# Prompt attention of a decoder step on one core: scaled scores from ScalarE, and another place for the weights' low part

## What is computed

```
z = (q @ k^T) / sqrt(HEAD_DIM) + bias
log_keep = where(mask, log_sigmoid(-z), 0)
suffix = cumsum(log_keep, reversed) - log_keep
attn = where(mask, exp(log_sigmoid(z) + suffix), 0)
o = attn @ v
proj = u @ w_in          # q and gate for all 16 heads, k and v from s @ w_k, s @ w_v
```

## Time and profile before

| | |
|---|---|
| Median of three runs | 1843.4 us |
| The profiled execution: its time | 1843.44 us |
| Its span from first to last instruction | 1841.7 us |
| TensorE busy | 1746.1 us, 95% of the span |
| VectorE busy | 1137.3 us, 62% |
| ScalarE busy | 822.4 us, 45% |
| Granted TensorE clock, mean | 0.983 |

### The profile page before, as it was taken

One profiled execution on the slowest core, in us unless ns is written; L12 is line 12 of the kernel. 1 busy time (PEld: TensorE's weight loads), 2 busy tenths in 40 slices (PEclk: granted clock), 3 DMA queues, 4 the chain that ended last, 5 costly groups with the idle time before them and its releaser, 6 DMA issues.

```text
span 1841.7 us, 35650 instructions
## 1 busy us (share of the span) xinstructions
PE 1746.1 (95%) x14063; PEld 1674.6 (91%) x14063; DVE 1137.3 (62%) x1917; ACT 822.4 (45%) x1246; POOL 230.8 (13%) x173
## 2 busy tenths in 40 slices
PE   6999999999999999996898999999998999999997
PEld 5999999999999999994898989989987888899996
DVE  4766555676567422229578788787876666642366
ACT  4434444344445222224255655655664555622343
POOL 2000000000000000011232222322321111001111
PEclk9999999999999999998999999999998999999997
DMA  8322332332322332335222222222213777622465
GB/s 247 107 83 78 91 89 82 91 93 78 91 80 69 87 90 86 85 106 179 83 82 58 76 63 64 76 63 58 86 48 110 210 229 221 196 75 86 134 182 189
DMA packets 293526, 197.98 MB, mean 107 GB/s; under 512 B 8379, under 2 KB 267579, under 8 KB 293307
## 3 DMA queue, kind: packets, MB, share of 16 engines
q1 hardware_dynamic: 290632, 187.36, 34.9%
q0 software_dynamic: 2720, 8.78, 1.3%
q10 hardware_dynamic: 68, 0.41, 0.1%
HBM read 180.55 MB, written 15.97 MB: 107 GB/s over the span
## 4 chain that ended last, share of the span: by engine, by line
PE 79%; DVE 10%; issue 5%; ACT 4%; DMA 1%; SPq 0%; ACTq 0%; POOL 0%; DVEq 0%
PE PS L720 22%; PE PS L722 22%; PE PS L721 22%; PE Z L983 2%; PE Z L720 1%; PE Z L722 1%; PE Z L721 1%; PE Z L993 1%; DVE WS L1657 1%; DMA xin<-in_x_prompt_dram 1%; DVE T L1953 1%; DVE T L1954 1%; PE Z L1017 1%; ACT T L1387 1%; PE Z L1176 1%
## 5 line engine op out<-in xcount | busy, mean ns | idle before, releaser
L720 PE MATMUL PS<-U,WS 128*128 128x272 f32 x3680 | 1078.1, 293 | 28.4 <-DVE U L1920 14.0
L722 PE MATMUL PS<-U,WS 128*128 128x272 f32 x3680 | 1067.6, 290 | 0.0
L721 PE MATMUL PS<-U,WS 128*128 128x272 f32 x3680 | 1065.1, 289 | 0.0
L720 PEld LDWEIGHTS PS<-U,WS 128*128 128x128 f32 x3680 | 697.1, 189 | 42.5 <-issue 22.3
L721 PEld LDWEIGHTS PS<-U,WS 128*128 128x128 f32 x3680 | 696.9, 189 | 0.9
L722 PEld LDWEIGHTS PS<-U,WS 128*128 128x128 f32 x3680 | 696.1, 189 | 0.0
L1657 DVE TENSOR_TENSOR WS<-raw,WS 128x1024 fp32r<-128x1024 f32 (+1 forms) x223 | 298.0, 1337 | 368.3 <-ACT WS L1208 365.8
L1208 ACT ACTIVATE WS<-raw 128x1024 fp32r<-128x1024 f32 (+1 forms) x225 | 230.7, 1025 | 479.4 <-PE PS L722 478.8
L633 POOL TENSOR_TENSOR raw<-raw,GN 128x1024 f32<-128x1024 f32 x80 | 158.0, 1975 | 583.5 <-DMA raw<-in_b_w_in_dram 486.7
L642 POOL COPY T<-T 128x544 f32<-128x544 f32 x2 | 1.7, 862 | 611.9 <-ACT T L1347 562.3
L1407 ACT ACTIVATE U<-T 128x256 fp32r<-128x256 f32 (+1 forms) x64 | 31.9, 499 | 88.5 <-DVE T L1972 88.5
(11 more groups left out here) (286 smaller groups left out, 2070.8 us busy)
## 6 DMA issues: line engine op xcount, KB each, us to landing
raw<-in_a_w_in_dram SPq DMA_DIRECT2D x80, 512.0 KB, 3.8
raw<-in_b_w_in_dram SPq DMA_DIRECT2D x64, 512.0 KB, 4.1
raw<-in_a_w_out_dram SPq DMA_DIRECT2D x32, 512.0 KB, 3.9
KPG<-in_cache_k_dram SPq DMA_DIRECT2D x64, 256.0 KB, 3.0
raw<-in_b_w_out_dram SPq DMA_DIRECT2D x32, 512.0 KB, 3.9
VPG<-in_cache_v_dram SPq DMA_DIRECT2D x60, 256.0 KB, 3.0
RAW<-in_b_w_out_dram SPq DMA_DIRECT2D x12, 512.0 KB, 4.7
scratch_x<-T POOLq DMA_DIRECT2D x16, 272.0 KB, 3.5
```

Of the source, the lines that this page charges most:

```text
L720: pe.matmul(psum, w_hi, x_hi, start=first, stop=False)
L721: pe.matmul(psum, w_hi, x_lo, start=False, stop=False)
L722: return pe.matmul(psum, w_lo, x_hi, start=False, stop=last)
```

## The change

Two edits. On ScalarE, `exp_logits` gets a fourth operation: behind Abs, an Identity with the same scale and bias writes z to T[:, 0] and raises `z_out`. VectorE's `scaled` is gone, with its wait for `z_abs`. In VectorE's `step`, `low` moves from in front of `mask_weights` to behind `at_rest` and in front of `sp_rest`.

```diff
-                nc.scalar.activation(T[:, 1, q], Z[:, 0, s % 2, q], ACT.Abs, scale=SCALE,
-                                     bias=BIAS[:, k * GRP + g:k * GRP + g + 1]).then_inc(z_abs, 1)
+                bias = BIAS[:, k * GRP + g:k * GRP + g + 1]
+                nc.scalar.activation(T[:, 1, q], Z[:, 0, s % 2, q], ACT.Abs, scale=SCALE, bias=bias).then_inc(z_abs, 1)
+                nc.scalar.activation(T[:, 0, q], Z[:, 0, s % 2, q], ACT.Identity, scale=SCALE, bias=bias).then_inc(z_out, 1)
                 act.wait_ge(z_abs, n + 1)
...
-            def scaled(k, g, s):
-                n = k * 16 + 4 * g + s
-                q = slice(FIRST_Q[s], SEQ)
-                dve.wait_ge(z_abs, n + 1)
-                if n:
-                    dve.wait_ge(l_ready, n)
-                V.tensor_scalar(T[:, 0, q], Z[:, 0, s % 2, q], SCALE, BIAS[:, k * GRP + g:k * GRP + g + 1],
-                                ALU.mult, ALU.add).then_inc(z_out, 1)
-
...
                 if before:
                     exponent(*before)
-                if s == 0:
-                    scaled(k, g, 0)
-                if next_unit is not None:
-                    low(D0 + next_unit, next_unit % 2)
-                if before:
                     mask_weights(*before)
                 if s == 1 and (k or g):
                     head_out(*((k, g - 1) if g else (k - 1, GRP - 1)))
                 softplus(k, g, s)
                 if before:
                     at_rest(*before)
+                if next_unit is not None:
+                    low(D0 + next_unit, next_unit % 2)
                 sp_rest(k, g, s)
-                if s < 3:
-                    scaled(k, g, s + 1)
```

## The result

The changed kernel takes 1861.94 us (four runs, 1861.46 to 1862.86 us), the kernel before 1845.43 us on the same chip (four runs, 1842.26 to 1849.64 us). The ratio is 1.0085 (slower by 0.85%), 95% interval 1.0063 to 1.0106. The forecast was 1851.8 us with a range of 1837 to 1861: the sign was that of the sum, the size was about half, and the time lies outside the range. The two profiled executions have spans of 1841.7 and 1861.1 us, 19.4 us apart. Where those lie is read from them.

A forecast was written before the change was run, and what follows sets the result against it. The prediction took TensorE, 95% busy, as the bound, with 25.0 us of its waits on VectorE's order. Terms 4.0 + 3.5 + 2.4 - 1.5 = +8.4 us on the median 1843.4 gave 1851.8 us, range 1837 to 1861.

The forecast's parts named there:

- The ceiling of 29.1 us: TensorE's whole idle time in the steps from 924 to 1392 us, claimed as the most any gain there could be.
- `scaled` goes: VectorE loses 64 operations, 37 us of its time; in steps s > 0 the next operation begins up to 0.75 us earlier.
- Identity comes: ScalarE's added copy delays Ln and softplus by 0.35 to 0.55 us and gives ScalarE 27 us more work.
- rival 4: Identity on ScalarE needs another table, loaded twice in each of 64 steps: 2007 us at worst, chance 0.02.
- `low` moves, the open wait: VectorE idles 0.5 us per step before the mask; chain from `exponent` to `sp_rest` grows from 4.17 to 4.41 us.
- The fold: GpSimd's fold moves with `low` onto softplus and `at_rest`: 0 to 1.9 us lost per unit, minus 0.55 saved.
- two-step units: Eight units holding two steps: first wait gone, later ones added by folds, net +0.5 us each, +4.0 us in all.
- gate units: Units ending a gate strip: `low` now stands in the open behind the mask, `later` waits about 1 us; +3.5 us in all.
- the steps s = 0: 16 steps where Abs to Ln is no longer covered by `low` and a fold can fall in: +2.4 us.
- Loads ... priced at nothing: Weight slots come free up to 3 us later, but some 2.5 us of reserve before `high` was taken to absorb it.
- Rival 3: Weight loads become the bound: some 20 of 55 units slip by 0.7 us, +14 us on top, 1866 us; chance 0.08.
- Rival 1: Faster: folds fall beside VectorE's chain or do not stop softplus, -7.7 us, 1835.7 us; chance 0.2.

## Why the prediction was half right

- **The bound and the ceiling.** TensorE's path and the waits for VectorE were the right place. The ceiling of 29.1 us was one of idle time at the granted clock and left out that the clock can fall behind waits.
- **`scaled` goes.** Right that it starts `exponent` earlier: L909 fell from 9.8 to 2.5 us with this edit alone. The move alone does as much (2.3 us), and both give 0.5. What the edit is worth was seen too small: alone it gives 10 us, where only the 0.75 us in front of the next `exponent` was weighed.
- **Identity comes.** Estimated at 0.35, 0.45 and 0.55 us of ScalarE's chain; starts are 0.36, 0.46 and 0.57 us apart (the unit of 1047.44, 1060.31 and 1125.25 us). ScalarE got 20.5 us in the steps where 27 stood. No table load came with it, so rival 4 falls; the Trainium skill's filler rule (ScalarE: Activation LUTs, Table sets) agrees.
- **`low` moves, the open wait.** Priced at 0.5 us, seen as 0.52 us of idle time (0.83 us at 1063.14 us, where `high` stands in front on ScalarE). The chain was put at 4.41 us; in a unit without a fold on it, it takes 4.75 us (1061.88 to 1066.63). The name of the wait changed as described, L901 from 4.1 to 21.4 us against "20 or more". But L923 was to fall under 4 us and stayed at 9.7.
- **The fold.** Right in mechanism and place. Softplus's operations with both inputs in SBUF are stopped as `tensor_tensor` is. The row, with the fold beside it, is below. Over the steps the mean of `low` fell from 1763 to 1340 ns, that of softplus's first operation rose from 515 to 677, `sp_rest` from 577 to 830. But as waits the folds cost TensorE no more than before (22.0 us of idle time against 23.3, each kernel against its run without folds); what they added came through the clock.

```profile
1079.84 2.14 DVE L1945 SCALAR_TENSOR_TENSOR T<-T 128x256 f32<-128x256 f32 x1 [1.19 <-ACT T L1392]
```
```profile
1079.78 1.91 POOL L633 TENSOR_TENSOR raw<-raw,GN 128x1024 f32<-128x1024 f32 x1 [7.60 <-DMA raw<-in_b_w_in_dram]
```

  By the Trainium skill (SBUF — State Buffer, Who interferes with whom) two SBUF inputs are enough; the trace agrees, 2.14 us for 0.42.
- **The sum.** In terms of waits it was too high by about 3 us, with its largest term right. Added up over the timeline, the waits in two-step units went from 19.9 to 24.4 us, +4.5 against +4.0. The gate units' own waits and the `rest` behind them gave +0.7 against +3.5, the steps s = 0 +0.6 against +2.4, and a wait of 0.7 us made by a fold in the first head went (against -1.5). All waits in the steps: +5.0 us against +8.4. The gate units' wait itself was seen rightly: put at about 1 us, it is 0.73 to 0.94 us in the seven of them. That the total comes near the forecast's is in part luck: it is the difference of Identity's gain of 10 us and a move that costs 26 beside it, and neither was priced as such.
- **The step that failed first: the clock.** The sum has no term for TensorE's speed, and took the earlier trace rows's 1.00 as given. 13.7 us more at the lower level are up to 6.8 us, of 7.3 us of busy time, more than the added waits (4.7). The row to warn of it was there: the 2.17 us wait of the earlier trace rows is followed by the only such stretch in the steps before.
- **The step that failed second: the queue.** "Loads ... priced at nothing" looked at the reserve of the weight slots only. What stands behind the waiting load on SyncE, the first key pages, wasn't asked. It costs 5.7 us of wait and, by the profiles, 6.3 us of span; the run with early key pages gives 5.5 us of time back. Rival 3 was near this place with another mechanism, and that one did not come: VectorE's `low` waited for `high` for 0.0 us in the changed kernel.
- **Added up.** Ahead of the steps +1.2 us, idle time in them +4.7, busy time +7.3, behind them +6.3: 19.5 against 19.4 us of span. The +1.2 belongs to neither edit: the first step's `qk` starts anywhere from 919.6 to 922.9 us in the runs here. The medians of the comparison are 16.5 us apart; the clock's falls differ from execution to execution, and the split is that of the profiled one.
- Rival 1 (faster) needed less than 0.5 us of each fold on the chain. The means of the mask, softplus's three operations and both low parts, less those of the kernel without folds, add up to 1.1 us for each fold; in the kernel before it was 0.3 us, and `low` took 0.5.

## To carry to other kernels

An operation that frees a buffer starts what comes after it: moving it moves the load, everything queued behind that load on the same queue, and the next engine's work on the tile, so follow it until it meets the critical chain again. Where two engines exclude each other, look first for the order in which they meet; here one wait on GpSimd is worth 12 us, and taking the meeting away altogether was worth 30 to the kernel before. And price a new wait of TensorE of a microsecond or two at more than itself if the profile shows the granted clock falling behind one like it.

## What was not expected of the hardware

- Idle stretches of TensorE of 1.7 to 2.4 us within a few microseconds, single waits or two with some matmuls between, were followed in four places of the changed kernel by 3.4 or 6.8 us at half the clock. By idle time in the steps: the three runs with 7 to 15 us have 0 to 3.4 us at the lower level, the seven with 21 to 31 us have 3.4 to 10.2, the four with 33 to 41 us have 17.1 to 34.1.
- The folds, 1.97 us each and off every critical path by themselves, cost the kernel before 26 us of its steps and 30 us of its time, since VectorE's small operations queue behind them.
- A VectorE operation of 0.29 us was recorded with 3.08 us where GpSimd issued stores and then a fold. With the stores alone it takes 0.29 us. Why it is held before the fold's record begins stays open.
